# Two halves of a PSUM bank added to h one by one, POOL's sums of squares one output later, and two weight splits moved behind the chain at the ends of down projections

## The reference

```
h = h + mixer(rms_norm(h, g_mix))            # MLA + forgetting attention, short convolution,
                                             # differential attention, mLSTM
h = h + square(relu(rms_norm(h, g_mlp) @ w_up)) @ w_down      # 1024 -> 4096 -> 1024
...
rms_norm(x, g) = x * rsqrt(mean(x * x) + 1e-6) * g
```

## Time and profile before

| | |
|---|---|
| median of 3 runs | 1310.88 us (1310.67 to 1315.07) |
| the profiled execution, its own time | 1308.48 us |
| its span | 1306.8 us |
| PE busy | 1244.7 us, 95% |
| DVE busy | 915.3 us, 70% |
| ACT busy | 710.0 us, 54% |
| POOL busy | 259.1 us, 20% |
| granted TensorE clock, mean | 0.983 of full speed |

### The profile page before, as it was taken

One profiled execution on the slowest core, in us unless ns is written; L12 is line 12 of the kernel. 1 busy time (PEld: TensorE's weight loads), 2 busy tenths in 40 slices (PEclk: granted clock), 3 DMA queues, 4 the chain that ended last, 5 costly groups with the idle time before them and its releaser, 6 DMA issues.

```text
span 1306.8 us, 24299 instructions
## 1 busy us (share of the span) xinstructions
PE 1244.7 (95%) x8344; PEld 1128.9 (86%) x8344; DVE 915.3 (70%) x1571; ACT 710.0 (54%) x1275; POOL 259.1 (20%) x277
## 2 busy tenths in 40 slices
PE   7999999999999999999999889999999978999996
PEld 5988889999999888888899668888889866888885
DVE  5778875555557988765666788776658858877563
ACT  4647656654444556644454666664445845666441
POOL 3000022210101134410100013440007501443010
PEclk9999989999999999999999899999999988999997
DMA  7414235655546556555565215655554422565540
GB/s 215 147 41 150 78 116 164 192 175 179 193 157 198 179 176 193 193 171 197 179 195 194 65 60 171 188 193 193 188 166 142 155 92 75 183 192 193 187 135 33
DMA packets 202390, 205.70 MB, mean 157 GB/s; under 512 B 6080, under 2 KB 199734, under 8 KB 202314
## 3 DMA queue, kind: packets, MB, share of 16 engines
q1 hardware_dynamic: 200053, 203.12, 48.7%
q10 hardware_dynamic: 2260, 1.58, 0.5%
HBM read 203.61 MB, written 1.06 MB: 157 GB/s over the span
## 4 chain that ended last, share of the span: by engine, by line
PE 76%; DVE 13%; ACT 5%; issue 3%; POOL 1%; DMA 0%; DVEq 0%; SPq 0%; POOLq 0%; ACTq 0%
PE PS L1550 28%; PE PS L1551 14%; PE PS L1544 9%; PE PS L1545 9%; PE PS L1546 9%; DVE wlo L886 4%; DVE x L863 2%; DVE tmp L907 1%; ACT whi L469 1%; DVE h L917 1%; PE PS L1765 1%; PE PS L1700 1%; PE PS L1743 1%; POOL mt L1520 1%; POOL mqk L1523 1%
## 5 line engine op out<-in xcount | busy, mean ns | idle before, releaser
L886 DVE TENSOR_TENSOR wlo<-raw,whi 128x1024 fp32r<-128x1024 f32 x370 | 451.7, 1222 | 211.2 <-ACT whi L469 209.5
L469 ACT ACTIVATE whi<-raw 128x1024 fp32r<-128x1024 f32 x370 | 388.2, 1053 | 325.3 <-PE PS L1551 211.4
L1550 PE MATMUL PS<-x,whi 128*128 128x512 f32 x832 | 292.3, 395 | 4.9 <-DVE x L863 4.5
L1544 PE MATMUL PS<-x,whi 128*128 128x256 f32 (+2 forms) x928 | 269.8, 291 | 9.8 <-DVE x L863 5.5
L1545 PE MATMUL PS<-x,whi 128*128 128x256 f32 (+2 forms) x928 | 267.6, 288 | 0.0
L1550 PE MATMUL PS<-hid,whi 128*128 128x512 f32 x768 | 267.0, 394 | 0.0
L1546 PE MATMUL PS<-x,wlo 128*128 128x256 f32 (+2 forms) x928 | 265.3, 286 | 0.0
L1551 PE MATMUL PS<-x,wlo 128*128 128x256 f32 x832 | 234.4, 282 | 0.0
L1551 PE MATMUL PS<-hid,wlo 128*128 128x256 f32 x768 | 212.7, 277 | 0.0
L1451 POOL TENSOR_TENSOR acc<-acc,sq 128x256 f32<-128x256 f32 (+2 forms) x72 | 63.9, 887 | 705.1 <-ACT sq L507 704.0
L1550 PEld LDWEIGHTS PS<-x,whi 128*128 128x128 f32 x832 | 156.3, 188 | 42.2 <-DVE x L863 6.8
(11 more groups left out here) (288 smaller groups left out, 1640.6 us busy)
## 6 DMA issues: line engine op xcount, KB each, us to landing
raw<-in_mlp_w SPq DMA_DIRECT2D x64, 1024.0 KB, 5.3
raw<-in_w_mlp_up SPq DMA_DIRECT2D x32, 1024.0 KB, 5.5
raw<-in_w_mlp_down SPq DMA_DIRECT2D x32, 1024.0 KB, 4.9
raw<-in_w_in_conv SPq DMA_DIRECT2D x12, 1024.0 KB, 5.2
raw<-in_attn_w_in SPq DMA_DIRECT2D x12, 1024.0 KB, 5.1
raw<-in_mlstm_w_in SPq DMA_DIRECT2D x12, 1024.0 KB, 5.3
raw<-in_w_in_attn SPq DMA_DIRECT2D x9, 1024.0 KB, 5.2
raw<-in_w_out_attn SPq DMA_DIRECT2D x4, 1024.0 KB, 5.5
```

The costliest lines, as they stand in the source:

```text
L469: A(part_view(whi, b), raw_view(b), ACT.Copy).then_inc(w_hi, 1)
L886: V.tensor_tensor(part_view(wlo, b), raw_view(b), f32(part_view(whi, b)), ALU.subtract).then_inc(w_lo, 1)
L1544: mm(dst, whi_b, xs_hi, start=first, stop=False)
L1550: mm(dst.rearrange("p (a t) -> p a t", a=2), std_cols(whi[b % RING], k), xs_both, start=first, stop=False)
```

## The change

Three edits.

In the output projections with paired products (n = 3, 5, 7), the reduce over both halves and the add to h become two adds: the first half of the bank and h into `tmp`, then the second half and `tmp` into h. The bank is released by the second add, which is also what ACT's `residual` waits for now (`out_h` is gone).

```
 # out_proj, DVE
-                        halves(tmp[:, j % 2, 0:S], bank(stage, j)).then_inc(psum_read, 1)
-                        dve.wait_ge(psum_read, O[stage] + j + 1)
-                        V.tensor_tensor(at(h, j, tok), tmp[:, j % 2, 0:S], at(h, j, tok), ALU.add).then_inc(Z["out_h"], 1)
+                        b = bank(stage, j)
+                        V.tensor_tensor(tmp[:, j % 2, 0:S], PS[:, b, 0:S], at(h, j, tok), ALU.add).then_inc(Z["out_half"], 1)
+                        dve.wait_ge(Z["out_half"], KB * (n // 2 - 1) + j + 1)
+                        V.tensor_tensor(at(h, j, tok), PS[:, b, S:2 * S], tmp[:, j % 2, 0:S], ALU.add).then_inc(psum_read, 1)
 # out_proj, ACT
-                    residual(n, j, tok, (psum_read, O[stage] + j + 1) if n == 1 else (Z["out_h"], KB * (n // 2 - 1) + j + 1))
+                    residual(n, j, tok, (psum_read, O[stage] + j + 1))
```

```
 # sums, POOL
                 def add(k, i=0):
+                    if n in (3, 5, 7) and k < KB - 1:
+                        pool.wait_ge(w_used, B[("c_out", "d_out", "m_out")[n // 2 - 1]] + k + 2)
+                    elif n in (2, 4, 6) and k < 3:
+                        pool.wait_ge(w_used, i * 16 + (B[f"dn{n // 2 - 1}"] + (8, 15, 16)[k]))
```

```
 # down, DVE
-                        if j < 15:
+                        if j % 8 < 6:
                             split_lo(B[dn] + 16 * c + j + RING, r, 16)
-                        if j % 8 >= 6:
+                        else:
                             low_part(2 * m + 2, o, tok, r)
-                    split_lo(B[dn] + 16 * c + 15 + RING, r, 16)
+                        if j % 8 == 7:
+                            split_lo(B[dn] + 16 * c + j - 1 + RING, r, 16)
+                            split_lo(B[dn] + 16 * c + j + RING, r, 16)
```

More of the change, by code:

```diff
@@ L253, in build @@
         names = """w_hi w_lo w_used psum_read const_in vec_in x_in lam_in_s rel_in rel_out mask_in hankel_in sel_in
-            relu_done dn_scaled out_h cs_ready const_set pool_set pro_t pro_ev h_ready x_hi x_ready sq_ready acc_ready norm_mm norm_ln norm_read rstd_ready
+            relu_done dn_scaled out_half cs_ready const_set pool_set pro_t pro_ev h_ready x_hi x_ready sq_ready acc_ready norm_mm norm_ln norm_read rstd_ready
             y_hi y_ready hid_hi hid_sq hid_ready dve_step out_n out_t out_left out_right out_sent
```

## The result

The changed kernel takes 1307.32 us (median of 20 executions, 1305.54 to 1311.49); the kernel before took 1311.26 beside it (20, 1308.34 to 1315.78). The ratio is 0.997, with an interval of 0.9961 to 0.998: 3.9 us faster. The sum was 6.65. The time lies inside the forecast range and above the likeliest case's own range (to 1306.0), at the figure that rival (b) had, and it is the same within half a per cent.

What follows compares the result with a forecast made beforehand. TensorE's matmuls were taken to bound the kernel, with three 2.05 us stalls on x7. 6.15 plus 0.5 gave 6.65 us, from the 1310.88 median to 1304.2 us; range 1301 to 1309.

Steps and rivals of the forecast that it cites:

- The sum: Whole kernel: 6.15 us from three output projections plus 0.5 us from ends of down projections, 6.65 us faster.
- the likeliest case: Whole kernel: gain of 5 to 7.5 us, own range 1303.0 to 1306.0 us, chance 0.62.
- rival (b): Up projections: half of the 6.15 us comes back as waits for split blocks, 1307.3 us; chance 0.20.
- The bound: Whole kernel waits for TensorE's matmuls; PE loses 2.05 us on x7 behind each of three paired output projections.
- Edits 1 and 2: Paired output projections: halves added directly to h, POOL adding one output later; 2.05 us gained at three places, 6.15 us.
- Rival (a): Output projections: low part stays at 0.96, or POOL holds the adds by 0.48; 1305.1 or 1304.9 us, chance 0.13.
- Edit 3: Ends of down projections: splits go behind the second output's chain, 0.5 us faster together.
- the 0.24 per end: Ends of down1 and down2: low part starts at 648.68, last reduce at 649.08 instead of 649.32, gain 0.24 us each.
- the +0.5: Ends of down1 and down2: together 0.5 us gained, with bounds of 0 and 0.9.
- The price of edit 3: Down projections: first deferred block ready 4.7 us after DVE could read the bank, wanted at 5.35, margin 0.65.
- rival (c): Pairs inside down projections: deferred splits, held three times by 0.48, stall PE at 12 places; 1313.7 us, chance 0.05.

Runs made afterwards that it cites:

- e3: Kernel before with only POOL adding one output later in the output projections, reduce and add to h as before: 1307.99 us, ratio 0.9972.
- e4: Kernel before with only the splits put behind the chains of down projections, POOL adding as before: 1316.79 us, ratio 1.0044.
- e1: Kernel before with the two adds and POOL one output later in the output projections, down projections as before: 1307.79 us, ratio 0.9969.
- e8: Changed kernel without the deferred splits, POOL's waits kept everywhere: 1306.87 us, ratio 0.9969.
- e10: Kernel before with the two adds and POOL's later add in d_out and m_out only, not c_out: 1306.44 us, ratio 0.9958.

## Why the prediction was right, and where wrong

**The bound, right.** PE waited for the low part at three places, the stall at each was 2.05 us, and 2.16 came back: the 2.05, and 0.11 by which the first matmuls behind the stall were slower. Nothing else became late there, and rival (b), waits for split blocks in the up projection, did not happen: the up stages show no row of it and are 2.16 shorter in full. That the median lies at (b)'s 1307.3 is a coincidence of numbers; what took the gain is elsewhere.

**Edits 1 and 2, right in each step.** Forecast 0.46 to the second add, 0.34 more, the low part at 0.48, 2.00 us from the end of the last output to chunk 7, margin 0.25; measured 0.46, 0.42 long as the nearest row had it, 0.48, and no wait. Either edit alone nearly suffices, as worked out (2.83 and 2.60 us per output against PE's 2.80): up stages at 90.09 and 89.97. Rival (a) failed in both halves: POOL's adds held no add that reads PSUM, and it was POOL that had held the low part, as e3 shows by moving POOL alone.

The Trainium skill ("VectorE: DVE Perf Modes", The DRAIN you can't avoid) as the prediction took it would have had DVE fall behind by 0.06 per output and the output projections at 5.6 instead of 6.15. The trace disagrees with that: the low part starts at 465.90 beside the split's 464.76 + 1.23 = 465.99, and the last first-add is 0.20 behind PE, where seven times 0.06 would have made it 0.6. The same section of the Trainium skill goes on to say that a next operation that is not held starts earlier, which the prediction left out; with that the trace agrees.

**Edit 3, wrong, and the step that failed is its first.** It said that the low part, freed of the split in front of it, would start at 648.68, 0.04 after ACT's part. DVE at the end of dn1 in the changed kernel, and the matmul that waits, against the earlier trace rows:

```profile
649.15 0.48 DVE L863 SCALAR_TENSOR_TENSOR x<-h,vec_b,x  x1 [1.09 <-ACT x L503]
649.55 0.68 DVE L907 TENSOR_REDUCE tmp<-PS 128x256 f32<-128x512 f32 x1
```

```profile
652.91 0.38 PE L1551 MATMUL PS<-x,whi 128*128 128x256 f32 x1 [1.38 <-DVE x L863]
```

ACT's part starts at 648.37 and takes 0.51, so the low part comes 0.27 after it. It had come 0.28 after it before too (648.92 against 648.13 + 0.51), with the split filling just that time. The 0.04 was taken from the output projection (471.14 + 0.51 to 471.68), which is written out; the down projection is a loop. The kernel before already had the longer figure: at 652.14 nothing stood in front of the low part, and ACT's part had ended at 651.87:

```profile
651.36 0.51 ACT L503 ACTIVATE x<-h,vec_b  x1 [2.41 <-DVE h L961]
```

The scaling and the add to h speak for the loop as the reason: 0.46 between their starts in down3, which is written out, and 0.59 in down1:

```profile
650.04 0.43 DVE L860 TENSOR_TENSOR tmp<-tmp,rstd 128x256 f32<-128x256 f32 x1
650.63 0.43 DVE L961 TENSOR_TENSOR h<-tmp,h 128x256 f32 x1 [0.16 <-DVE tmp L860]
```

No run has the same stage in both forms with a low part in it. So the 0.24 per end that was forecast became nothing, and the +0.5 became 0: idle 1.38 instead of 1.37 (1.31 in e4, without the scaling held by POOL).

**The price of edit 3, wrong in size.** The block was forecast ready 4.7 us after DVE could read the bank, margin 0.65. At the pass boundary of dn1 the bank could be read at 603.62 (0.20 behind a block that starts two blocks ahead of 608.96, when the stalled one was due). The reduce came at 604.15, late by 0.53 and not by 0.22, for in front of it the low part had waited out the same 0.27. Then 2.82 and 0.40, as forecast, and a split of 1.8 instead of 1.23. That is 0.31 + 0.57 = 0.88 over the forecast, 0.23 over the margin, and PE's 609.19 is 0.23 behind 608.96. So by this sum neither the lag nor POOL alone makes PE wait, and both together do; no run takes the lag away. The prediction called POOL's adds "Nothing", having gone through them beside the chain and not behind it; rival (c) wanted three holds of 0.48 at 12 places, and what decides is one hold, at the few places that POOL's own wait doesn't clear. Nor is the 0.23 all. The next block takes 2.94 us, and those behind it 2.82 or 2.83 instead of 2.77 to the end of dn1, which makes most of its 1.08. In dn2 the same wait (0.41 on the weight load) is followed by one block of 2.88 and then by 2.77 again, so its loss stops at 0.36. Why the two differ stays open. In sum edit 3 is worth -1.44 us of stage time (and POOL's waits in the down projections -0.13) where +0.5 was forecast.

**The size of the whole.** 6.47 - 1.44 - 0.13 = 4.9; by the means 4.4 were measured, 4.8 at equal clock. The forecast had no term for the clock. In the changed kernel that term is small (0.4), but in e1 and e8, which leave the mistake out, it is 1.0 to 1.1 by the fit. That is part of why neither beats it clearly; at equal clock e8 is 0.9 ahead of it and e1 0.3, where the stages give 1.4 and 1.6, and the rest stays open. The trace that the sum was made against was also a short one, 1308.48 with a mean clock of 0.983, where the kernel's mean is 0.981. The best version measured is e10, 5.1 us under the kernel before, and its interval (0.9943 to 0.9974) takes in the changed kernel's 0.997. That the time landed at 1307.3 inside the range was in part luck: the losses by edit 3 and by the clock had no term.

**The Trainium skill** ("GPSIMD Engine Reference", Specifications) puts the contention on DVE instructions with two SBUF inputs. The traces agree: the new adds, with one PSUM input, are 0.42 with POOL beside them; low part, split, scaling and the add to h at the end of dn0, with two SBUF inputs, were all held.

## What to carry to other kernels

Take the lag between a wait's release and its instruction from rows of the same program part, loop or written out, before pricing a move that shortens the queue in front of it. When an instruction with two SBUF inputs is moved, look for POOL at its new place, to a quarter of a microsecond. And before a change of 2 us is judged by the median of a kernel with lulls in TensorE's work, compare the mean clocks of the executions: a few thousandths are worth as much as the change.

## What the runs showed of the hardware

- Of a POOL add and a DVE instruction with two SBUF inputs that overlap, the second to start is held: the low part takes 0.96 instead of 0.48 when it starts 0.12 after POOL's add, the first of two splits 0.54 more when it starts 0.21 after.
- In the loops of the down projections the low part, when it waits for ACT, starts 0.27 to 0.30 us after ACT's part has ended; in the output projections, which are written out, 0.03.
- The mean clock of one and the same kernel runs from 0.974 to 0.987 between executions: 38 executions of the kernel before at 0.983 or more have a mean of 1310.6 us, 13 at 0.977 or less 1315.6.
- After one wait of PE in a down projection its blocks can stay at 2.82 us instead of 2.77 (dn1 of the changed kernel, to the stage's end, at a granted clock of 1.00) or come back to 2.77 after one block (dn2 of the same execution). Why stays open.
- A stretch of low clock costs by where it falls: ahead of a wait for another engine it is hidden in the wait (0.98 instead of 1.95 us of it in m_in), and one late in the attention goes with about 2 us more (d_in and d_out at 141.0 to 141.3 instead of 138.7 to 139.3).
